# Weights of 32 experts in runs of 16 KB instead of 8 KB, with the gathered rows' places turned and the first loads in another order

## The reference, cut to what matters

```python
h = layer_norm(x, ln0_g, ln0_b)
mix = token_mixer(h, w_in, conv_w, a_log, dt_bias, gdn_norm_w, sinks, w_o)
h = layer_norm(ALPHA * h + mix, ln1_g, ln1_b)
# hierarchical_moe: group top-1, then expert top-2 inside it
def expert_block(args):
    xblk, e = args
    hdn = silu(xblk @ w_gate[e]) * (xblk @ w_up[e])
    return hdn @ w_down[e]
...
y = segment_sum(yb * row_w[:, None], row_tok, num_segments=T)
h = layer_norm(ALPHA * h + y, ln2_g, ln2_b)
```

## Time and profile before

| | us |
|---|---|
| median of three runs | 1969.11 |
| lowest and highest run | 1962.87, 1969.8 |
| the profiled execution's own time | 1964.93 |
| its span in the profile | 1963.3 |
| TensorE busy | 1834.9 (93%) |
| VectorE busy | 1020.9 (52%) |
| ScalarE busy | 633.6 (32%) |
| GpSimd busy | 363.9 (19%) |
| weights' DMA issues | 384 of 1024 KB |

### The profile page before, as it was taken

One profiled execution on the slowest core, in us unless ns is written; L12 is line 12 of the kernel. 1 busy time (PEld: TensorE's weight loads), 2 busy tenths in 40 slices (PEclk: granted clock), 3 DMA queues, 4 the chain that ended last, 5 costly groups with the idle time before them and its releaser, 6 DMA issues.

```text
span 1963.3 us, 25311 instructions
## 1 busy us (share of the span) xinstructions
PE 1834.9 (93%) x10346; PEld 1107.6 (56%) x10346; DVE 1020.9 (52%) x1713; ACT 633.6 (32%) x1044; POOL 363.9 (19%) x293
## 2 busy tenths in 40 slices
PE   5999999999999998999999999898889988899996
PEld 4778877887788776888733333333333333333332
DVE  6456655665552555433645545445454544444456
ACT  6323332333243555112323331323323132232324
POOL 0334323432343231454000000000000000000001
PEclk9999999999999998999899999999999999999998
DMA  7322222312232212535899999999999999999996
GB/s 258 86 65 77 54 65 65 83 48 65 65 95 65 65 62 76 213 114 188 314 398 421 420 420 420 421 420 420 421 420 415 416 418 416 413 400 405 419 409 283
DMA packets 173317, 505.45 MB, mean 257 GB/s; under 512 B 19697, under 2 KB 109937, under 8 KB 120721
## 3 DMA queue, kind: packets, MB, share of 16 engines
q1 hardware_dynamic: 168256, 494.76, 65.3%
q0 software_dynamic: 4944, 9.05, 1.2%
HBM read 498.92 MB, written 13.76 MB: 261 GB/s over the span
## 4 chain that ended last, share of the span: by engine, by line
PE 58%; DMA 30%; DVE 7%; ACT 2%; issue 2%; SPq 1%; POOL 0%; POOLq 0%; DVEq 0%; ACTq 0%
DMA ring<-in_w_up 27%; PE bank L2370 11%; PE bank L1949 10%; PE bank L1950 9%; PE bank L1951 9%; PE bank L2379 4%; PE bank L2345 2%; DMA ring<-in_w_down 2%; DVE half L1330 2%; PE bank L2096 1%; PE bank L2087 1%; PE bank L2105 1%; DVE att L1536 1%; DVE sc L1531 1%; DVE sc L1551 1%
## 5 line engine op out<-in xcount | busy, mean ns | idle before, releaser
L2370 PE MATMUL bank<-ring,xbT 128*64 128x512 f32 x2048 | 475.7, 607 | 62.6 <-DMA ring<-in_w_up 59.8
L725 POOL TENSOR_TENSOR wlo<-raw,whi 128x512 fp32r<-128x512 f32 x232 | 312.4, 1378 | 524.8 <-ACT whi L851 370.3
L1784 DVE TENSOR_TENSOR r<-r,bank 128x512 f32<-128x512 f32 x464 | 287.5, 682 | 201.9 <-PE bank L2345 201.9
L2370 PEld LDWEIGHTS bank<-ring,xbT 128*64 128x64 f32 x2048 | 153.8, 139 | 339.1 <-issue 338.5
L1949 PE MATMUL bank<-hTh,wlo 128*128 128x512 f32 x704 | 299.0, 425 | 2.0 <-DVE hTl L1263 1.2
L1950 PE MATMUL bank<-hTl,whi 128*128 128x512 f32 x704 | 276.5, 393 | 0.0
L1951 PE MATMUL bank<-hTh,whi 128*128 128x512 f32 x704 | 276.4, 393 | 0.0
L2379 PE MATMUL bank<-ring,hidT 128*64 128x512 f32 x984 | 218.2, 595 | 0.6 <-issue 0.5
L771 POOL DMA_INDIRECT xb<-h_scr,idx_tok x32 | 31.7, 991 | 860.2 <-PE bank L2357 850.3
L1789 DVE TENSOR_TENSOR yhl<-yw,yhl 64x512 fp32r<-64x512 f32 x120 | 82.8, 690 | 201.2 <-ACT yhl L1159 198.4
L851 ACT ACTIVATE whi<-raw 128x2048 fp32r<-128x2048 f32 x50 | 95.7, 1913 | 198.9 <-PE bank L1951 198.9
(11 more groups left out here) (357 smaller groups left out, 2013.9 us busy)
## 6 DMA issues: line engine op xcount, KB each, us to landing
ring<-in_w_gate SPq DMA_DIRECT2D x128, 1024.0 KB, 27.9
ring<-in_w_up SPq DMA_DIRECT2D x128, 1024.0 KB, 27.6
ring<-in_w_down SPq DMA_DIRECT2D x127, 1024.0 KB, 26.8
raw<-in_w_in SPq DMA_DIRECT2D x44, 1024.0 KB, 5.7
raw<-in_w_o SPq DMA_DIRECT2D x16, 1024.0 KB, 5.1
xt<-in_x SPq DMA_DIRECT2D x4, 1024.0 KB, 8.9
h_scr<-xt SPq DMA_DIRECT2D x4, 1024.0 KB, 7.9
r<-h_scr SPq DMA_DIRECT2D x1, 4096.0 KB, 12.6
```

The lines of the kernel that those rows point to most:

```text
L725: i = pool.tensor_tensor(wlo[sl][:, part, :], raw[sl][:, :].rearrange("p (k n) -> p k n", k=KD)[:, part, :], whi[sl][:, part, :].bitcast(F ...
L1784: dve.tensor_tensor(v, v, comb_bank(q, tt)[:, :], ALU.add).then_inc(comb_done, 1)
L2370: i = mm(GU[SLOTS * h:SLOTS * (h + 1), :], xT_[:, k, :], w[:, kk * F:(kk + 1) * F], start=k == 0, stop=k == KD - 1)
```

## The change

Gate and up are now fetched in DMAs of 2 MB, 16 KB in each partition (`pair`): the pieces of steps 0 and 1, and of steps 2 and 3. Down is divided otherwise: a partition holds two neighbouring rows of down, so that two parts lie together in 16 KB (`h p c`), and the hidden rows are turned with a stride of two columns to match. There are seven places of 16 KB, six from the 155th turn on, and two single places (`once`) for the last two down pieces of the first expert. The first expert's gate and up of a step share one place and are still fetched in pieces of 8 KB, so are the first gate and up halves of the second expert (`first`, `second`); the last expert's last two down pieces are fetched apart.

The four pieces of the second expert are issued before the stores of the normalised rows; the first expert's last two pieces come after them, the first of the two when the pool engine has issued the first gather (`fetch_issued`, raised by a small memset behind it).

The place of a rank is looked up in a new table of 64 constants: place 8a + c stands for rank 8((c - 2(a div 2)) mod 8) + a.

Of the three unread products before the first expert one is left.

```diff
-RING = 15
-SHORT, SHORT_FROM = 12, 300
+RING = 7
+SHORT, SHORT_FROM = 6, 154
...
+    a_, c_ = np.divmod(np.arange(SLOTS), 8)
+    r[:, R_SLOT:R_END] = ((c_ - 2 * (a_ // 2)) % 8 * 8 + a_)[None, :]
...
-    down_v = w_down[0].rearrange("e (c p) n -> p e c n", p=P)
+    down_v = w_down[0].rearrange("e (h p c) n -> p e h c n", h=2, p=P)
...
-            return 8 * t + (i // 2 + 1 if i < 8 else i - 3)
+            if t == 0:
+                return (1, 2, 3, 4, 6)[i]
+            return 8 * t + (2, 2, 4, 4, 6, 8)[i]
...
+            def pair(e, i):
+
+                h, j = divmod(i, 2)
+                if h < 2:
+                    return [gate_v, up_v][j][:, e:e + 1, h:h + 1, :, :].rearrange("p o h k f -> p (o h k f)")
+                return down_v[:, e:e + 1, j:j + 1, :, :].rearrange("p o h c n -> p (o h c n)")
...
+            first(6, 8)
+            second(6, 1, 1)
+            second(5, 0, 1)
+            sp.wait_ge(strip_mm, STRIPS + PIECES)
+            first(7, 9)
+            second(6, 1, 0)
+            second(5, 0, 0)
+            row_store(0, l1_norm, 2)
+            row_store(1, l1_gain, TT + 1)
+            row_store(2, l1_gain, TT + 2)
+            row_store(3, l1_norm, 3)
+            sp.wait_ge(fetch_issued, 1)
+            first(10)
+            sp.wait_ge(logits, LG_B)
+            first(11)
...
+            for m in range(NPAIR + 2, NPAIR * E - 1):
+                t, i = divmod(m, NPAIR)
+                r = ring_slot(m)
+                sp.wait_ge(w_used, used_when(ring_before(m)))
+                sp.dma_start(ring[r][:, :], pair(ORD[t], i)).then_inc(w_loaded[r], 16)
+                if turn(m) == SHORT_FROM + 2 * SHORT:
...
-            for t in range(2):
-                gather(t)
+            gather(0)
+            pool.memset(slot_tw[:, 0:1], 0.0).then_inc(fetch_issued, 1)
+            gather(1)
...
-                step(dve.tensor_tensor(slot_oh[:, js, :].rearrange("p j (a b) -> p j a b", a=8),
-                                       tokens[:, 0:SLOTS].rearrange("p (o b a) -> p o a b", o=1, b=8).broadcast_to([P, n, 8, 8]),
-                                       pos[:, ts, :].rearrange("p t (c o q) -> p (t c) o q", o=1, q=1).broadcast_to([P, n, 8, 8]),
+                step(dve.tensor_tensor(slot_oh[:, js, :], rc[:, R_SLOT:R_END].rearrange("p (o s) -> p o s", o=1).broadcast_to([P, n, SLOTS]),
+                                       pos[:, ts, :].rearrange("p t (c o) -> p (t c) o", o=1).broadcast_to([P, n, SLOTS]),
                                        ALU.is_equal))
...
-            unread(3)
+            unread(1)
...
+            hid_c = hid[:, :].rearrange("s (h p c) -> s h c p", h=2, c=2)
...
-                    i = by(HT_PS[:, c * SLOTS:(c + 1) * SLOTS], hid[SLOTS:P, c * P:(c + 1) * P],
+                    i = by(HT_PS[:, c * SLOTS:(c + 1) * SLOTS], hid_c[SLOTS:P, c // 2, c % 2, :],
...
+                        if kg_ % 2 == 0:
+                            pe.wait_ge(w_loaded[r_g], n_g)
+                            pe.wait_ge(w_loaded[r_u], n_u)
```

More of the change, by code:

```diff
@@ L231, in build @@
         raw_at, hi_at, lo_at = ([ST + 8 * KB * (2 * j + i) for i in range(2)] for j in range(3))
[L232 to L235, removed]
+        ring_at = [mx_hi[0], mx_lo[0], raw_at[0], mx_hi[2], mx_lo[2], lo_at[0], hi_at[0]]
+        ring = [at(f"ring{i}", ring_at[i], [P, 8 * F]) for i in range(RING)]
+        once = [at(f"once{i}", GD + 16 * KB * i, [P, 4 * F]) for i in range(2)]
         yw = at("yw", GD, [P, 4, F])
@@ L418, in build @@
         scattered = sem("scattered")
-        w_loaded = [sem(f"w_loaded{i}") for i in range(RING + 1)]
+        w_loaded = [sem(f"w_loaded{i}") for i in range(RING)]
+        fetch_issued = sem("fetch_issued")
+        once_loaded = [sem(f"once_loaded{i}") for i in range(2)]
+        end_loaded = [sem(f"end_loaded{i}") for i in range(2)]
         w_used = sem("w_used")
@@ L651, in weight_source, with place_of, first, second @@
                     return src.rearrange("p o h k f -> p (o h k f)")
-                return down_v[:, bass.ds(e, 1), i - 8:i - 7, :].rearrange("p o c n -> p (o c n)")
+                h, c = divmod(i - 8, 2)
+                return down_v[:, bass.ds(e, 1), h:h + 1, c:c + 1, :].rearrange("p o h c n -> p (o h c n)")
+            def pair(e, i):
[3 more added lines that the diff above has]
+                return down_v[:, e:e + 1, j:j + 1, :, :].rearrange("p o h c n -> p (o h c n)")
+            def place_of(c):
+                return once[c - 10][:, :] if c >= 10 else ring[c // 2][:, 4 * F * (c % 2):4 * F * (c % 2) + 4 * F]
+            def first(*cs):
+                for c in cs:
+                    sp.dma_start(place_of(c), piece(ORD[0], c)).then_inc(once_loaded[c - 10] if c >= 10 else w_loaded[c // 2], 16)
+            def second(r, i, h):
+                sp.dma_start(ring[r][:, 4 * F * h:4 * F * h + 4 * F], piece(ORD[1], 2 * h + i)).then_inc(w_loaded[r], 16)
             def row_store(t, done, n):
@@ new lines, in _ @@
+            sp.wait_ge(strip_mm, STRIPS + PIECES - 3)
+            first(0, 2)
+            sp.wait_ge(strip_lo, STRIPS + PIECES - 1)
+            first(5)
+            sp.wait_ge(strip_mm, STRIPS + PIECES - 2)
+            first(1, 3)
+            sp.wait_ge(strip_lo, STRIPS + PIECES)
+            first(4)
+            sp.wait_ge(strip_mm, STRIPS + PIECES - 1)
+            first(6, 8)
[3 more added lines that the diff above has]
+            first(7, 9)
@@ new lines, in _ @@
+            second(6, 1, 0)
[8 more added lines that the diff above has]
+            first(11)
+            sp.wait_ge(rt, RT_FLAG)
+            most = sp.value_load(ovi[0:1, 2 * LEFTOVER + 1:2 * LEFTOVER + 2], min_val=0, max_val=S)
+            with sp.If(most > SLOTS):
+                sp.wait_ge(rt, RT_ALL)
+                left = sp.value_load(ovi[0:1, 2 * LEFTOVER:2 * LEFTOVER + 1], min_val=0, max_val=LEFTOVER)
+                for r in range(RING):
+                    sp.wait_ge(w_loaded[r], 32)
+                for i in range(2):
+                    sp.wait_ge(once_loaded[i], 16)
+                with sp.Fori(0, left) as lf:
+                    e = sp.value_load(ovi[0:1, bass.ds(lf, 1)], min_val=0, max_val=E - 1)
+                    sp.wait_ge(lf_dve, LF_DVE * lf + LF_START)
+                    for c in range(NPIECE):
+                        sp.dma_start(place_of(c), piece(e, c)).then_inc(lf_w, 16)
+                sp.wait_ge(lf_dve, LF_DVE * left + LF_START)
+                for c in range(NPIECE):
+                    sp.dma_start(place_of(c), piece(ORD[0], c)).then_inc(lf_w, 16)
@@ L697, in _ @@
+            sp.wait_ge(w_used, used_when(ring_before(NPAIR * E - 1)))
+            for c in range(2):
+                sp.dma_start(ring[r][:, 4 * F * c:4 * F * c + 4 * F], piece(ORD[E - 1], 10 + c)).then_inc(end_loaded[c], 16)
             for t in range(2):
@@ L2423, in block_pe @@
                     for kk in range(4):
-                        i = gate_up(xbT[t % 2], 4 * kg_ + kk, ring[r_g], ring[r_u], kk)
+                        i = gate_up(xbT[t % 2], 4 * kg_ + kk, *((w, at_ + kk) for w, at_ in weights))
                     i.then_inc(w_used, 1)
```

127 lines of the change are left out of this document (51 added, 76 removed).

## The result

The changed kernel takes 1940.8 us (median of four runs, 1939.83 to 1943.17) where the kernel before, on the same chip, takes 1966.38 (a fourth run beside the three of the table): a ratio of 0.9873, 95% interval 0.9855 to 0.9892. In a second set of runs it took 1938.49 beside 1964.42, ratio 0.9867 (0.9852 to 0.9882). The profiled execution has a span of 1941.5 us. The forecast was 1937 with a range of 1924 to 1956.

The account below looks back on a forecast made before the run. The weight stream bounds the expert stage: 980.6 + 22.83 x 30.16 + 2 gives 1671 us, remaining pieces and ln2's loads 1902, last hidden row 1909.5, tail 24.6 gives 1934, 1.6 around it 1936. Forecast set at 1937, range 1924 to 1956.

Parts of the forecast that it names:

- (a) Places: Gathered rows' place table: alternating filled places evens the DMA engines' load, saving 0.76 us per expert, possibly nothing.
- (b) Runs: Weight loads in 16 KB runs: half the packets save 1.4%, 0.42 us per expert, uncertain from 0 to 1.5.
- (c) Start: Before the first expert: reordered loads and fewer unread products free the first place 2.5 us sooner, between 0.5 and 4.
- (e) Coarser places: Weight places of 2 MB: one more step (3.5 us) at the end, starving of the stream costed at nothing.
- (f) Stride: Hidden rows' transposes read every second column: 0 to 2.5 us in the last five experts, taken as 0.
- The end: After the last weights: last hidden row at 1909.5 us, then an unchanged 24.6 us to the span's end, 1934.
- The signs: Profile marks: first load about 980, 16 KB packets, period 30.2 us, constant excess, tensor engine without waits from expert 27.
- long runs that don't pay: Rival for the weight stream: balanced places work but 16 KB runs gain nothing, 13 us more, 1950 us; chance 0.17.
- places that don't matter: Rival for the row gather: long runs pay but balance doesn't, engines being unequal by themselves, 1956 us; chance 0.08.
- the starved stream: Rival for the weight places: they come back too late, one piece's time lost per expert, 1997 us; chance 0.03.
- the runs would pay in full: Rival for the weight stream: 16 KB runs gain 5%, tensor engine bounds from expert 26 on, 1927 us; chance 0.08.
- Neither: Rival: neither balance nor long runs pay, the extra step eats the start's gain, 1966 us; chance 0.09.

Follow-up runs that it names:

- the 4 KB kernel: Changed kernel with each 2 MB load issued as four of 512 KB, giving 4 KB runs; 1979.13 us, ratio 1.0074 to the kernel before.

## Why the prediction was right

Forecast: 1937 for 1940.8 and 1938.5 measured, 28 us of gain for 25.6 to 25.9. By its steps:

**What bounds.** Right: weights bound the middle of the expert stage, and the gain is a shorter period, 31.27 to 30.26.

**(a) Places.** Right in kind, too large in size: 0.76 us per expert reckoned, 0.45 to 0.55 measured (30.71 against 30.26, 31.16 against 30.69, 31.27 against 30.72). The term that was mis-sized is the 31.34 us of before set against a full stream's 30.58. But 31.34 is a mean over 7.83 experts' worth of pieces at 31.93 us (983.12 to 1233.26) and 15 at 31.03. With even places alone the 15 took 30.62 each, as good as the 30.58, so the gain there is 0.41. The early ones still took 31.39 (987.00, the first load, to 1232.91), and the queue's 99.75 MB in that time are 1.2 MB more than the complete pieces: they never got near 30.58. Nor is the lead all that uneven places cost; part of it is a stream that moves fewer bytes, 0.5% in the kernel before and 1.1% in the changed one.

**(b) Runs.** Right: 0.42 forecast, 0.43 measured, with the lower price, 8.5 ns a run in the reckoning and 9 by the three lengths. That it is right to the hundredth is luck. The price hung on 10 ns for a tiny packet, which no row of before gave, and zero and 5% were as open; the traces have 9 to 10 ns for these packets. The rule of the Trainium skill ("DMA: Bandwidth & Descriptors", Why small descriptors are slow) had been set beside it with 0.6% by its three cycles a packet (0.8% with the 32 bytes of descriptor that the same section adds, an estimate as well): the runs show 1.5%, about twice as much or more, and the measurement decides. The bound of 5% came from a share rounded to a tenth, and from tiny packets counted as free.

**(c) Start.** 2.5 us forecast; 3.6 from the gather's issue to the first step and 3.6 to the first load (980.14 - 970.86 = 9.3, before 983.12 - 970.24 = 12.9). The stores were in time, with some 3 us to spare: in the second profile the DMA share is 0.79 in 965 to 967.5 and 0.06 in the next 2.5 us, and the gather is issued at 970.86. That fewer products are needed for the earlier rows to count is shown (1.7 us of the 3.6); the wait for the gather's issue is worth 0.3, less than I had thought. The first profile hid the gain in the first load's time, 982.84, being 3.2 us late from before.

**(e) Coarser places.** No starving: the share is 1.01 and the stream at 427 GB/s. The one more step behind the last landing is there, 7.09 us of matmuls from 1912.51 where one step takes 3.65. With both main parts taken back the kernel is at 1.0008 of before, so what the start won was given back; by subtraction that falls to the coarser waits and the strided transposes together, and no kernel parts them.

**(f) Stride.** Taken as nothing, between 0 and 0.5 us per expert: it is 0.22 (0.69 for 0.47), about 1 us in the last five experts.

**The end.** The last activation was forecast for 1909.5 and came at 1919.6 in the profiled execution, 1916.5 in the second profile. The miss lies early. The first step of the 25th expert waits for two pieces more than the forecast's 1671, so for 1676; it was released at 1687.5. Of these 11 us 2.2 are the late start of the one execution. The rest is 23 experts' worth taken at 30.16 us: the first eight (982.84 to 1233.66) took 31.35, the next 15 30.25. The full stream begins later than I had it, since the first experts' loads are issued place by place: the share is 0.79 in 980 to 985, and in slices of 6.5 us the queues move 309 to 401 GB/s from 1005.6 to 1031.6. From 1687.5 to the last activation it was 232.1 us, forecast 233.5.

From the activation to the span's end it was 21.9 us instead of 24.6, which gave 2.7 back. I had taken that tail as fixed. The vector engine ends equally long after the activation in both (16.6 us), but in before the last scatter of rows waits for the last store of the output: issued at 1946.69, it holds the pool engine until 1956.92. After, that store is issued at 1928.36 and has landed by 1933.06, before the last rows are ready. Why it lands sooner is not shown.

So the span was forecast for 1934 and was 1941.5. That 1937 is only 1.5 to 3.8 us off the medians is in part luck: the tail gave 2.7 back, the profiled execution lay 2.4 above its median, and 1937 was set between the sum's 1936 and the 4.2 us of scatter beside it without a rule.

**The signs.** Those of the first load (980.14), the packets and the period came. Two did not: the excess still grows, and the tensor engine still waits behind ln2's loads (3.07 us) and once in the last expert (0.79).

The rivals: long runs that don't pay (1950) and places that don't matter (1956) each fell by a kernel of its own, the starved stream by the shares. That the runs would pay in full fell by the 4 KB kernel: the price per run is the same 9 ns at every length, which leaves nothing of the 5%. "Neither" fell by the ratio itself.

## What to carry to other kernels

When a stream is cut alike over all DMA engines, anything uneven beside it can set the pace: count the bytes moved against the bytes of complete loads, at two times far apart, and if the difference grows, or the rate falls in stretches, look for the small transfer that is laid on some partitions only. On a full queue price a layout by its number of contiguous runs, and get that price from rows of two lengths before believing a larger gain. Where two things end together, a shorter one of them brings little; look for what covers it.

## What the runs showed of the hardware that I had not expected

A gather of 0.26 MB beside 12.58 MB of weights cost 11 to 14 us of 1966 by the partitions that it wrote alone. The DMA share hardly tells: it stood at 1.01 while the lead was building up, and at 0.97 to 1.00 in stretches of 50 us later, where the bytes fell from 426 to 405 GB/s and from 420 to 398.

A run costs 9 ns of the pace beyond its bytes, at 4, 8 and 16 KB alike, on a queue that is never empty.

A stride of two costs little where the tensor engine reads (0.22 us for four transposes of 64 rows). Writing alternately to two places 128 elements apart costs much on the scalar and vector engines (518 and 370 ns for 64 x 512).
